# First attention interleaved with the 16 chunks of the attention gate and the recurrent output, tanh gates, queries laid out by fours

## The chip, the cores and the metric

The kernel runs on one core of a Trainium2 chip. The metric is the device time of one execution in microseconds (us), as the median of several runs. Engines are named as in the profile: PE (TensorE), DVE (VectorE), ACT (ScalarE), POOL (GpSimd), SP (SyncE, which only issues the loads here).

## The reference

A hybrid block for 256 tokens (with 16 meta tokens ahead of them T = 272), width 1024, and then a second block of two layers. Only the first half of the first block is touched:

```python
n1 = rmsnorm(h, norm1_g)
xr, gr, cq, ckv, kr, g_rnn, g_att = split(n1 @ w_in)
hr = rg_lru(causal_conv(xr))                        # linear recurrence over the tokens
y_rnn = (hr * gelu(gr)) @ w_rnn_out
q  = rmsnorm(cq)  @ w_uq                            # 16 heads, 64 nope + 32 rope
kv = rmsnorm(ckv) @ w_ukv                           # 16 heads, 64 key + 64 value
o  = causal softmax attention(q, k, v)              # rope on 32 of the 96 dims
y_att = o @ w_attn_out
mixed = sigmoid(g_rnn) * y_rnn + sigmoid(g_att) * y_att
h = h + mixed @ w_out
```

Behind it come a mixture over 16,384 experts (PEER) and the second block (four SwiGLU layers, a convolution module, an 8-head attention); they are the same before and after.

## The kernel before

All weights of all stages lie in one stream of 667 chunks of 128 x 1024 fp32 (512 KB each), in the order of `STAGES` (line 72). SP loads chunk c into slot c mod 3 of `raw`. ACT writes its rounded high half to `whi` (`split`, line 402) and DVE the remainder to `wlo` (`split`, line 830). PE then makes three passes per 128 x 128 tile (`passes`, line 1450): high times high, low activations, low weights. A chunk of a projection is 24 such matmuls into one PSUM bank (`chunk_out`, line 1463). PE adds one to `used` when it is done with a chunk, DVE adds one to `lo_done` when one is ready. Activations are split in the same way: ACT writes `XH`, DVE writes `XL`.

Every engine runs its own program in the written order, and the programs are tied by semaphores alone. The order around the change is: xr, ckv, kr, cq, gr (projections of n1), 16 small products for the recurrence gates, grnn (8 chunks, sigmoid on ACT, and between them on ACT and DVE the decay arithmetic of the recurrence, `decay`, line 542), gatt (8 chunks, beside them DVE's scans, line 1026), wro (recurrent output, 8 chunks), uq (queries: 16 heads of nine matmuls, line 597 on), uk (keys), uv (values), attention 1, wao (attention output), wout.

In uq a head's 128 outputs are 64 nope rows, 32 rope rows and the 32 rope rows turned. ACT copies the nope rows (line 571); DVE multiplies the rope rows by cosine (1049) and sine (1052) on 32 partitions and adds them (1054). POOL copies the rope rows of the keys for 16 heads (1881) behind the scans. In uv four banks of `wide` and two of `acc` collect the values; ACT copies them all out (585, 587) before attention begins. Projection outputs go through three banks `acc` in turn; `OUTS`, `EV` and `READ` (332 to 344) hold which engine has read each.

Attention 1 (1632 on PE, 1060 on DVE, 589 on ACT) treats a head as: two score matmuls (fp32, 96 rows; keys 144 and 272 wide), DVE adds the mask and takes the maximum (1072, 1077), ACT takes the exponential with its sum (598), DVE scales (1084, 1087), PE transposes five tiles (1656), ACT copies them (608, 610), PE multiplies by the values (1671). PE's order is scores(h+1), turn(h-1), values(h-2). No chunk is worked on meanwhile.

## Time and profile before

| | |
|---|---|
| median of 3 runs | 2295.47 us (2293.35 to 2297.09) |
| the profiled execution's own time | 2295.11 us |
| its span, first to last instruction | 2293.3 us |
| PE busy | 2184.4 us, 95% |
| DVE busy | 1548.8 us, 68% |
| ACT busy | 1189.1 us, 52% |
| first attention, on the trace's clock | about 227.4 to 322.3 us |

How to read it: all times in rows are microseconds from the span's start, unless marked ns. Busy time of PE counts a pipelined matmul from its start to its modelled end, so successive matmuls overlap; their rate is seen in the distance of their starts. PEclk is the clock that PE was granted, as a share of 2.4 GHz; 0.5 is 1.2 GHz. "Idle before" is followed by the instruction that ended most of the idle time.

### The profile page before, as it was taken

Reading aid. Unit: us, or ns where it says so; the run is one execution under the profiler, and the core shown is the slowest. Engines: PE = TensorE matmul, PEld = TensorE weight load, DVE = VectorE, ACT = ScalarE, POOL = GpSimd, SP = SyncE. Lnnn points to the kernel's source line nnn. Section 1 sums busy time; section 2 is a strip of 40 time slices with the busy share of each in tenths; the row PEclk is TensorE's granted clock in tenths of the full one; section 3 lists DMA queues with packets and bytes.
Section 4 is the critical chain, followed back from the end, with each engine's and each line's share of the span. In section 5 each row is a group of like instructions: output and inputs, shape, how many; then the busy total and the mean of one; then the engine's idle time right before and its main releaser. Section 6 shows DMA issues by size and latency. Waiting matters only on the chain.

```text
span 2293.3 us, 42218 instructions
## 1 busy us (share of the span) xinstructions
PE 2184.4 (95%) x15056; PEld 1976.8 (86%) x15056; DVE 1548.8 (68%) x2607; ACT 1189.1 (52%) x2009; POOL 52.1 (2%) x77
## 2 busy tenths in 40 slices
PE   7997899999999999999999999989999999979998
PEld 7896468999999998888888999978998999868997
DVE  6577445599989996555556666776666666656666
ACT  4765334565657675555555445535445444545444
POOL 0010000000010000000002000000000000000000
PEclk9999569999999999999999999999999999989999
DMA  5453015454543335555555666404554555424554
GB/s 197 151 171 117 1 52 176 151 182 168 185 160 120 128 127 187 194 193 193 194 193 175 236 223 205 148 28 166 187 183 152 193 184 182 165 74 137 185 186 142
DMA packets 100974, 366.35 MB, mean 160 GB/s; under 512 B 11488, under 2 KB 12000, under 8 KB 100384
## 3 DMA queue, kind: packets, MB, share of 16 engines
q1 hardware_dynamic: 97632, 352.46, 45.5%
q0 software_dynamic: 3264, 12.85, 1.5%
q8 instruction: 49, 0.80, 0.1%
q14 instruction: 29, 0.24, 0.0%
HBM read 363.16 MB, written 2.10 MB: 159 GB/s over the span
## 4 chain that ended last, share of the span: by engine, by line
PE 75%; DVE 13%; issue 5%; ACT 5%; DVEq 1%; DMA 0%; ACTq 0%
PE acc L1453 13%; PE acc L1455 12%; PE acc L1454 12%; PE wide L1756 8%; PE wide L1757 8%; PE wide L1758 8%; DVE wlo L834 2%; DVE arena L1239 2%; DVE res L1225 2%; ACT whi L413 1%; PE wide L1572 1%; PE wide L1574 1%; PE wide L1573 1%; PE sums L1671 1%; PE acc L1828 1%
## 5 line engine op out<-in xcount | busy, mean ns | idle before, releaser
L1453 PE MATMUL acc<-XH,whi 128*128 128x256 f32 (+1 forms) x3088 | 885.1, 287 | 16.1 <-DVE wlo L834 10.1
L1454 PE MATMUL acc<-XL,whi 128*128 128x256 f32 (+1 forms) x3088 | 874.9, 283 | 0.0
L1455 PE MATMUL acc<-XH,wlo 128*128 128x256 f32 (+1 forms) x3088 | 874.6, 283 | 0.0
L839 DVE TENSOR_TENSOR wlo<-raw,whi 128x1024 fp32r<-128x1024 f32 x396 | 484.8, 1225 | 302.5 <-ACT whi L418 282.5
L1453 PEld LDWEIGHTS acc<-XH,whi 128*128 128x128 f32 x3088 | 592.2, 192 | 28.3 <-DVE wlo L834 10.7
L1454 PEld LDWEIGHTS acc<-XL,whi 128*128 128x128 f32 x3088 | 592.5, 192 | 3.0
L1455 PEld LDWEIGHTS acc<-XH,wlo 128*128 128x128 f32 x3088 | 592.4, 192 | 0.0
L418 ACT ACTIVATE whi<-raw 128x1024 fp32r<-128x1024 f32 x456 | 479.8, 1053 | 181.3 <-PE wide L1758 181.0
L834 DVE TENSOR_TENSOR wlo<-raw,whi 128x1024 fp32r<-128x1024 f32 x268 | 328.1, 1227 | 171.2 <-ACT whi L413 160.6
L1756 PE MATMUL wide<-whi,small 128*128 128x512 f32 x864 | 338.4, 392 | 6.5 <-DVE wlo L834 3.6
L1757 PE MATMUL wide<-whi,small 128*128 128x512 f32 x864 | 337.8, 391 | 0.0
L1758 PE MATMUL wide<-wlo,small 128*128 128x512 f32 x864 | 336.6, 390 | 0.0
L413 ACT ACTIVATE whi<-raw 128x1024 fp32r<-128x1024 f32 x208 | 217.7, 1052 | 112.0 <-PE wide L1574 40.5
L1756 PEld LDWEIGHTS wide<-whi,small 128*128 128x128 f32 x864 | 162.8, 188 | 39.0 <-DVE wlo L834 4.4
L1758 PEld LDWEIGHTS wide<-wlo,small 128*128 128x128 f32 x864 | 162.6, 188 | 34.7
L1757 PEld LDWEIGHTS wide<-whi,small 128*128 128x128 f32 x864 | 162.9, 189 | 30.6
L706 ACT ACTIVATE arena<-arena 128x256 f32<-128x256 f32 x88 | 36.8, 418 | 193.2 <-DVE arena L1297 193.2
L712 ACT ACTIVATE small<-arena 128x256 fp32r<-128x256 f32 x88 | 36.7, 418 | 178.8 <-DVE arena L1306 178.8
L656 ACT ACTIVATE last_parts<-res,r2T 128x128 bf16<-128x128 bf16 x256 | 81.7, 390 | 58.3 <-DVE res L1225 58.3
L631 ACT ACTIVATE arena<-acc 128x256 f32 (+1 forms) x79 | 30.3, 383 | 93.8 <-PE acc L1455 93.6
L1308 DVE TENSOR_TENSOR small<-arena,small 128x256 fp32r<-128x256 f32 x88 | 37.6, 427 | 42.5 <-ACT small L712 42.5
L1297 DVE TENSOR_TENSOR arena<-acc,rstd 128x256 f32<-128x256 f32 x88 | 37.4, 425 | 39.8 <-PE acc L1455 39.4
(266 smaller groups left out, 2258.3 us busy)
## 6 DMA issues: line engine op xcount, KB each, us to landing
raw<-stream SPq DMA_DIRECT2D x664, 512.0 KB, 3.3
arena<-taps_in POOLq DMA_DIRECT2D x20, 256.0 KB, 4.0
arena<-rows_in POOLq DMA_DIRECT2D x7, 512.0 KB, 4.4
arena<-h_in SPq DMA_DIRECT2D x2, 544.0 KB, 4.4
res<-rgw SPq DMA_DIRECT2D x1, 1024.0 KB, 8.6
res<-tokens_in POOLq DMA_DIRECT2D x1, 1024.0 KB, 5.3
park<-res POOLq DMA_DIRECT2D x1, 1024.0 KB, 4.4
res<-park POOLq DMA_DIRECT2D x1, 1024.0 KB, 5.6
```

The source lines that it names most:

```text
L413: act.activation(whi[:, c % RING, :], raw[:, c % RING, :], ACT.Copy).then_inc(hi_done, 1)
L418: act.activation(whi[:, c % RING, :], raw[:, c % RING, :], ACT.Copy).then_inc(hi_done, 1)
L656: ins = act.activation(last_part(m % 2)[:, a, :], of_group(onehots, m % 2, 0)[:, a, 0, :], ACT.Copy, scale=r2T[:, bass.ds(4 * g + a, 1)])
L834: V.tensor_tensor(wlo[:, c % RING, :], raw[:, c % RING, :], whi[:, c % RING, :].bitcast(F32), ALU.subtract).then_inc(lo_done, 1)
L839: V.tensor_tensor(wlo[:, c % RING, :], raw[:, c % RING, :], whi[:, c % RING, :].bitcast(F32), ALU.subtract).then_inc(lo_done, 1)
L1225: V.tensor_tensor(pairs(onehots[:, s, 0, :]), of_tokens(e12, g), pairs(iotab[:, :]).to_broadcast([P, 8, NK // 2, 2]), ALU.is_equal)\
L1453: mm(out_, whi[:, s, w], xh, start=first, stop=False, **kw)
L1454: mm(out_, whi[:, s, w], xl, start=False, stop=False, **kw)
L1455: return mm(out_, wlo[:, s, w], xh, start=False, stop=last, **kw)
L1756: mm(dst, xh[:, x], whi[:, c % RING, w], start=first, stop=False, skip_group_check=True)
L1757: mm(dst, xl[:, x], whi[:, c % RING, w], start=False, stop=False, skip_group_check=True)
L1758: ins = mm(dst, xh[:, x], wlo[:, c % RING, w], start=False, stop=last, skip_group_check=True)
```

## The change

- The stream's order becomes grnn, uq, uk, uv, gatt, wro. The ckv norm moves into grnn; its halves lie in `small`, not in `XH` and `XL`.
- A loop of 18 steps replaces gatt, wro and attention: in step p PE does chunk p of the 16 of gatt and wro, then scores(p+1), turn(p-1) and values(p-2). ACT and DVE have the matching order. Scores alternate between two banks of `wide` (head 0 uses `sums`), transposes use the other two, values always use `sums`. The recurrent product y is written over `GR`, and its halves are made in step 7.
- The scans of the recurrence run in uv (two) and in steps 0 to 5.
- sigmoid(x) becomes (tanh(x/2) + 1)/2: ACT computes tanh, DVE adds one within its product, and the factor 0.5 is applied when `wout` is added to the residual.
- The weights of uq are laid out so that four heads give one output of 4 x 32 rope rows, one of the same rows turned, and two of 2 x 64 nope rows. DVE multiplies the first two on 128 partitions and adds four times on 32; ACT copies the other two. Cosine and sine tables are repeated on 128 partitions, which adds one constant load (128 KB).
- Key copies go to ACT and DVE by turns; the middle part of the values is copied by DVE. POOL's rope copies of the keys start before the square root of the recurrence, not behind its scans.
- The storage in `arena` is laid out anew, and the second attention's code is written out for itself, with the same instructions.

```diff
-STAGES = [("xr", 8), ("ckv", 2), ("kr", 1), ("cq", 3), ("gr", 8), ("grnn", 8), ("gatt", 8),
-          ("wro", 8), ("uq", 6), ("uk", 2), ("uv", 2), ("wao", 8), ("wout", 8), ("wq", 16),
+STAGES = [("xr", 8), ("ckv", 2), ("kr", 1), ("cq", 3), ("gr", 8), ("grnn", 8), ("uq", 6), ("uk", 2),
+          ("uv", 2), ("gatt", 8), ("wro", 8), ("wao", 8), ("wout", 8), ("wq", 16),
...
+        def score_bank(h):
+            return sums[:, :] if h == 0 else wide[:, h % 2, :]
+
+        def uv_bank(q):
+            return (GO["gatt"] + 1 + q) % RING
...
-        CKH, CKL = xt(XH, 384, 2), xt(XL, 384, 2)
+        CKH = small[:, 0:768].rearrange("p (t n) -> p t n", n=384)
+        CKL = small[:, 768:1536].rearrange("p (t n) -> p t n", n=384)
         CQH, CQL = xt(small, SEQ, 3), cl
         norm("n1", h0, DT, T, "norm1", 0, XHT, XLT)
         norm("cq", CQ, 3, SEQ, "qn", 0, CQH, CQL)
-        xsplit("yin", DT, SEQ)
         norm("ckv", CKV, 2, T, "kvn", 0, CKH, CKL)
+        xsplit("yin", DT, SEQ, sem("gated_y"), GR)
...
-                             ("rg", 16, "A"), ("grnn", 8, "A"), ("gatt", 8, "A"), ("wro", 8, "V"),
-                             ("uq", H1, "V"), ("uk", 8, "A"), ("wao", 8, "V"),
+                             ("rg", 16, "A"), ("grnn", 8, "A"), ("uq", 16, "VVAA"), ("uk", 8, "AV"), ("gatt", 8, "A"),
+                             ("wro", 8, "V"), ("wao", 8, "V"),
...
+                if k == 1:
+                    do_norm("ckv", split_later=True)
                 if k == 4:
                     act.wait_ge(sem("u_sq"), 1)
                     act.activation(HR, HR, ACT.Sqrt, scale=-1.0).then_inc(sem("u_root"), 1)
-            lin("grnn", lambda k, ps: act.activation(SG[:, k, :], ps, ACT.Sigmoid), between=decay)
-            lin("gatt", lambda k, ps: act.activation(SA[:, k, :], ps, ACT.Sigmoid))
-            act.wait_ge(used, BASE["gatt"] + 8)
-            do_xsplit("yin")
-            do_norm("ckv", split_later=True)
-            for k in range(DT):
-                split(BASE["wro"] + k + AHEAD)
-                if k == 5:
                     norm_root("ckv")
-
-            act.wait_ge(used, BASE["wro"] + 8)
...
+            for n in range(16):
+                if n % 3 == 0:
+                    split(BASE["uq"] + n // 3 + AHEAD)
+                if n % 4 >= 2:
+                    act.wait_ge(*output_ready("uq", n, 3))
+                    m, h = bank("uq", n), 4 * (n // 4) + 2 * (n % 4 - 2)
+                    act.activation(Q1[0:64, h, :], m[0:64, 0:SEQ], ACT.Copy, scale=SCALE1)
+                    act.activation(Q1[0:64, h + 1, :], m[64:128, 0:SEQ], ACT.Copy, scale=SCALE1).then_inc(outputs_read["A"], 1)
+            act.wait_ge(used, BASE["uq"] + 6)
             do_xsplit("ckv")
...
+            exps(0)
             act.wait_ge(used, BASE["uv"] + 2)
-            for t in range(2):
-                act.activation(V1[:, t, :], wide[:, 2 * t:2 * t + 2, :], ACT.Copy).then_inc(sem("v1"), 1)
+            act.activation(V1[:, 0, :], wide[:, 0:2, :], ACT.Copy).then_inc(sem("v1"), 1)
             for q in range(2):
-                act.activation(V1[0:META, 2, q * 512:(q + 1) * 512], acc[q][0:META, :], ACT.Copy).then_inc(sem("v1"), 1)
+                act.activation(V1[0:META, 2, q * 512:(q + 1) * 512], acc[uv_bank(q)][0:META, :], ACT.Copy).then_inc(sem("v1"), 1)
+            b = BASE["gatt"]
+            for p in range(18):
+                if 1 <= p <= 8:
+                    act.wait_ge(used, b + p)
+                    act.activation(SA[:, p - 1, :], bank("gatt", p - 1)[:, 0:SEQ], ACT.Tanh, scale=0.5).then_inc(READ["gatt"], 1)
+                if p < 16:
+                    split(b + p + AHEAD)
+                if p == 7:
+                    act.wait_ge(used, b + 8)
+                    do_xsplit("yin")
+                if 1 <= p <= 16:
+                    turned_probs(p - 1)
+                if p < 15:
+                    exps(p + 1)
...
+                if k == 6:
+                    norm_x("ckv")
...
+            qt = arena[:, XN + 2 * T:XN + 2 * T + SEQ * 2].rearrange("p (t n) -> p t n", n=SEQ)
+            for n in range(16):
+                if n % 3 == 0:
+                    split(BASE["uq"] + n // 3 + AHEAD)
+                if n % 4 < 2:
+                    dve.wait_ge(*output_ready("uq", n, 3))
+                    if n >= 4:
+                        dve.wait_ge(sem("q1"), n // 4 * 4)
+                    V.tensor_tensor(qt[:, n % 4, :], bank("uq", n)[:, 0:SEQ], (cos4, sin4)[n % 4], ALU.mult)\
+                        .then_inc(outputs_read["V"], 1)
+                if n % 4 == 1:
+                    dve.wait_ge(*OUTS[GO["uq"] + n])
+                    for i in range(4):
+                        V.tensor_tensor(Q1[64:96, n // 4 * 4 + i, :], qt[32 * i:32 * i + 32, 0, :], qt[32 * i:32 * i + 32, 1, :],
+                                        ALU.add).then_inc(sem("q1"), 1)
+            x_lo("ckv")
...
+                if j % 2:
+                    dve.wait_ge(*output_ready("uk", j, 2))
+                    m = bank("uk", j)
+                    V.tensor_copy(K1[0:64, 2 * j, :], m[0:64, 0:T])
+                    V.tensor_copy(K1[0:64, 2 * j + 1, :], m[64:128, 0:T]).then_inc(outputs_read["V"], 1)
...
+            def scores(h):
+                dve.wait_ge(sem("a1sc"), h + 1)
+                for t in range(2):
+                    m = 2 * h + t
+                    s, w, at = m % 4, KEYS["a1"][t], 0 if t == 0 else META + P
+                    if h >= 2:
+                        dve.wait_ge(sem("a1ptr"), h - 1)
+                    V.tensor_tensor(PR[:, s, 0:w], score_bank(h)[:, at:at + w], mask1[:, t, 0:w], ALU.add).then_inc(sem("a1sr"), 1)
+                    dve.wait_ge(sem("a1sr"), m + 1)
+                    V.tensor_reduce(tiny[:, 8 + s:9 + s], PR[:, s, 0:w], AX, ALU.max, negate=True).then_inc(sem("a1negmax"), 1)
+
+            def probs(h):
+                for t in range(2):
+                    m = 2 * h + t
+                    s, w = m % 4, KEYS["a1"][t]
+                    dve.wait_ge(sem("a1exp"), m + 1)
+                    link(V.reciprocal(tiny[:, 48 + s:49 + s], tiny[:, 12 + s:13 + s]))
+                    V.tensor_scalar(PR[:, s, 0:w], PR[:, s, 0:w], tiny[:, 48 + s:49 + s], None, ALU.mult).then_inc(sem("a1pr"), 1)
+
+            def pair_out(g):
+
+                dve.wait_ge(sem("a1pv"), 2 * g + 2)
+                V.tensor_copy(O1[:, g, :], sums[:, 0:SEQ]).then_inc(sem("x_full"), 1)
+            scores(0)
+            only_split("uv")
+            scan(0)
+            scan(1)
+            probs(0)
+            dve.wait_ge(used, BASE["uv"] + 2)
+            V.tensor_copy(V1[:, 1, :].rearrange("p (a n) -> p a n", a=2), wide[:, 2:4, :]).then_inc(sem("v1_middle"), 1)
+            b = BASE["gatt"]
+            for p in range(18):
+                if p < 15:
+                    scores(p + 1)
+                if p == 7:
+                    x_lo("yin")
+                if p < 16:
+                    split(b + p + AHEAD)
+                if p < 6:
+                    scan(p + 2)
+                if p >= 9 and p <= 16:
+                    k = p - 9
+                    dve.wait_ge(READ["grnn"], EV["grnn"] + DT)
+                    dve.wait_ge(used, b + p)
+                    V.scalar_tensor_tensor(out=SG[:, k, :], in0=SG[:, k, :], scalar=1.0, in1=bank("wro", k)[:, 0:SEQ],
+                                           op0=ALU.add, op1=ALU.mult).then_inc(READ["wro"], 1)
+                if p < 15:
+                    probs(p + 1)
+                if p >= 3 and p % 2:
+                    pair_out((p - 3) // 2)
...
+            for j in (6, 7):
+                pe.wait_ge(*OUTS[GO["uk"] + j])
+            pe.wait_ge(sem("q1"), H1)
+            pe.wait_ge(sem("k1_rows"), H1)
+
+            def scores(h):
+                if h >= 3:
+                    pe.wait_ge(sem("a1sr"), 2 * h - 2)
+                elif h >= 1:
+                    pe.wait_ge(sem("v1"), 1)
+                for t in range(2):
+                    w, at = KEYS["a1"][t], 0 if t == 0 else META + P
+                    ins = mm(score_bank(h)[:, at:at + w], Q1[0:96, h, t * P:(t + 1) * P], K1[0:96, h, 0:w], start=True, stop=True)
+                ins.then_inc(sem("a1sc"), 1)
+
+            def turn(h):
+                if h == 0:
+                    pe.wait_ge(sem("v1_middle"), 1)
+                else:
+                    pe.wait_ge(sem("a1pt"), h)
+                pe.wait_ge(sem("a1pr"), 2 * h + 2)
+                for t in range(2):
+                    m = 2 * h + t
+                    for kt in range(-(-KEYS["a1"][t] // P)):
+                        w = min(P, KEYS["a1"][t] - kt * P)
+                        at = (kt % 2) * SEQ + t * P
+                        ins = nc.tensor.transpose(wide[0:w, 2 + kt // 2, at:at + P], PR[:, m % 4, kt * P:kt * P + w], ident[:, :])
+                ins.then_inc(sem("a1ptr"), 1)
+
+            def values(h):
+                pe.wait_ge(sem("a1pt"), h + 1)
+                g, r0 = h // 2, (h % 2) * 64
+                if h == 0:
+                    pe.wait_ge(sem("a1sr"), 2)
+                    pe.wait_ge(sem("v1"), 3)
+                elif h % 2 == 0:
+                    pe.wait_ge(sem("x_full"), norms["o1"].full + g)
+                parts = [(0, P, 0, 2), (1, META, 0, 1), (1, P, 1, 1), (2, META, 1, 1)]
+                for n, (kt, w, t, nt) in enumerate(parts):
+                    ins = mm(sums[r0:r0 + 64, t * P:(t + nt) * P], V1[0:w, kt, h * 64:(h + 1) * 64],
+                             PT[0:w, h % 2, kt * SEQ + t * P:kt * SEQ + (t + nt) * P], start=kt == 0, stop=n in (1, 3),
+                             skip_group_check=True)
+                ins.then_inc(sem("a1pv"), 1)
+            scores(0)
             pe.wait_ge(sem("pad"), 2)
             tokens_out("uv", "ckv", [[wide[:, 0, :], wide[:, 1, :]], [wide[:, 2, :], wide[:, 3, :]],
-                                     [acc[0][:, :], acc[1][:, :]]], None)
-
-            def attention(tag, heads, nkt, n, Q, K, V, rows):
-                pr = ar(pr_at, n, 4) if tag == "a1" else ar(12288, n, 4)
-                pt = ar(pt_at, 768, 2) if tag == "a1" else ar(13312, 512, 2)
-                keys_of = KEYS[tag]
+                                     [acc[uv_bank(0)][:, :], acc[uv_bank(1)][:, :]]], None)
+            n1, b = norms["n1"], BASE["gatt"]
+            for p in range(18):
+                if p < 16:
+                    pe.wait_ge(lo_done, b + p + 1)
+                    free("gatt", p)
+                    if p in (1, 2):
+                        pe.wait_ge(sem("v1"), 3)
+                    hi, lo = (n1.hi[:, :, META:T], n1.lo[:, :, META:T]) if p < 8 else (XHS, XLS)
+                    chunk_out(bank("gatt", p)[:, 0:SEQ], b + p, hi, lo, "yin" if p == 8 else None).then_inc(used, 1)
+                if p < 15:
+                    scores(p + 1)
+                if 1 <= p <= 16:
+                    turn(p - 1)
+                if p >= 2:
+                    values(p - 2)
...
-            pool.wait_ge(sem("lru_done"), DT)
+            pool.wait_ge(sem("u_sq"), 1)
...
-    uq = np.concatenate([uq, turned(uq[..., NOPE:])], axis=-1).reshape(QL, H1 * P)
+    rope = uq[..., NOPE:].reshape(QL, 4, 4 * ROPE)
+    swapped = turned(uq[..., NOPE:]).reshape(QL, 4, 4 * ROPE)
+    uq = np.concatenate([rope, swapped, uq[..., :NOPE].reshape(QL, 4, 4 * NOPE)], axis=-1).reshape(QL, H1 * P)
```

## Rows read from the trace of the kernel before

**Rows 1.** the page: PE's granted clock in 40 slices, in tenths.

```profile
PEclk9999569999999999999999999999999999989999
```

**Rows 2.** windows by stage: us, busy of PE PEld DVE ACT POOL, PEclk, DMA.

```profile
100.20:129.20 29.00, 24.94 (x195) 24.32 (x193) 15.57 (x11) 26.89 (x29) 0.67 (x1) 0.94 0.41 146
129.20:152.50 23.30, 22.96 (x192) 22.76 (x192) 18.75 (x24) 10.46 (x17) 0.00 (x0) 1.00 0.60 204
152.50:177.10 24.60, 24.07 (x196) 23.91 (x197) 18.76 (x27) 13.19 (x21) 10.53 (x16) 1.00 0.53 172
177.10:205.00 27.90, 20.79 (x147) 17.95 (x145) 26.02 (x53) 12.04 (x24) 0.50 (x2) 1.00 0.32 109
205.00:215.90 10.90, 7.04 (x48) 6.16 (x48) 6.58 (x10) 8.37 (x20) 0.00 (x0) 1.00 0.40 133
215.90:227.40 11.50, 8.45 (x36) 6.68 (x36) 2.45 (x2) 4.95 (x7) 0.00 (x0) 1.00 0.35 115
227.40:322.30 94.90, 85.90 (x273) 43.23 (x273) 37.38 (x135) 34.61 (x106) 0.00 (x0) 0.56 0.00 1
```

**Rows 3.** timeline of PE (start, us): heads at either clock.

```profile
227.45 3.11 PE L1643 MATMUL wide<-arena 96*128 96x144 f32 x12 [3.05 <-ACT arena L587]
242.10 1.68 PE L1671 MATMUL acc<-arena 128*64 128x256 f32 x7
243.71 0.97 PE L1643 MATMUL wide<-arena 96*128 96x144 f32 x4
247.39 2.96 PE L1671 MATMUL sums<-arena 128*64 128x256 f32 x8
250.28 1.76 PE L1643 MATMUL wide<-arena 96*128 96x144 f32 x4
251.83 1.27 PE L1656 MATMUL acc<-ident,arena 128*128 128x128 f32 x5
```

**Rows 4.** timeline of PE: two chunk matmuls at the low clock.

```profile
323.05 0.41 PE L1481 MATMUL acc<-XH,wlo 128*128 128x256 f32 x1
323.26 0.41 PE L1480 MATMUL acc<-XH,whi 128*128 128x256 f32 x1
```

**Rows 5.** timeline of POOL and DVE: rope copies, subtractions, a reciprocal.

```profile
152.66 10.53 POOL L1881 COPY arena<-arena 32x272 f32<-32x272 f32 x16 [50.89 <-DVE arena L1026]
152.97 4.47 DVE L846 TENSOR_TENSOR XL<-arena,XH 128x256 fp32r<-128x256 f32 x8
174.77 1.85 DVE L856 RECIPROCAL rstd<-rstd 128x272 f32<-128x272 f32 x1
322.69 2.77 DVE L846 TENSOR_TENSOR XL<-arena,XH 128x256 fp32r<-128x256 f32 x8
```

**Rows 6.** groups by line, query stage: busy, mean ns, idle before.

```profile
L1453 PE MATMUL acc<-small,whi 128*128 128x256 f32 x48 | 14.9, 310 | 7.0 <-DVE arena L1052 6.4
L1052 DVE TENSOR_TENSOR arena<-acc,zone 32x256 f32<-32x256 f32 x14 | 6.0, 428 | 0.2
```

**Rows 7.** timeline of ACT in grnn; PE's first gate matmul.

```profile
103.30 0.39 ACT L554 ACTIVATE arena<-acc 128x256 f32<-128x256 f32 x1 [1.37 <-PE acc L1455]
103.58 2.02 ACT L545 ACTIVATE arena<-arena 128x2176 f32<-128x2176 f32 x1
...
117.09 1.28 ACT L554 ACT_TABLE_LOAD   x1
...
120.01 1.28 ACT L553 ACT_TABLE_LOAD   x1
...
129.17 0.39 PE L1453 MATMUL acc<-XH,whi 128*128 128x256 f32 x1 [0.52 <-DVE wlo L834]
```

**Rows 8.** windows around two changes of PE's clock.

```profile
116.00:119.60 3.60, 1.21 (x10) 1.22 (x11) 2.49 (x2) 3.57 (x5) 0.00 (x0) 1.00 0.09 15
119.70:123.00 3.30, 3.30 (x17) 3.30 (x17) 2.10 (x2) 3.27 (x4) 0.00 (x0) 0.50 0.43 154
242.60:245.90 3.30, 2.08 (x11) 1.11 (x10) 1.98 (x7) 0.76 (x3) 0.00 (x0) 1.00 0.00 0
```

314 lines of the change are left out of this document (143 added, 171 removed).

## The prediction

> **What bounds the kernel now.** I read the page first, then a table of windows over the stages that the change touches, then the PE instructions inside attention. The page says that PE is busy 95% of the span, and that its granted clock is 0.9 or 1.0 of full nearly everywhere [rows 1]: most of the 2293.3 us is TensorE at full rate, which only fewer or faster matmuls would shorten. The slices with clock 5 and 6 stand out. The windows [rows 2] place them: in the first attention (227.40 to 322.30, 94.9 us) PE is busy 85.90 us but at a mean clock of 0.56, so at the 1.2 GHz level for nearly all of it, while DVE (37.38) and ACT (34.61) are mostly idle and no weights are moved. The same rows show two smaller losses: the query projection (uq, 177.10 to 205.00) has PE busy 20.79 of 27.9 us beside a DVE busy 26.02, and the stage of values (215.90 to 227.40) PE busy 8.45 of 11.5. Everything after 322.3 is the same work in the same order, so the forecast is the sum over the 222.1 us from 100.2 to 322.3.
>
> **Attention between chunks.** Per head PE does three groups. At the low clock the starts in [rows 3] give: values 247.39 to 250.28, 2.89 us; scores 250.28 to about 251.95, 1.67; five transposes from 251.83, 1.1. That is 5.65 us a head, times 16 is 90.4 of the 94.9; the rest is waiting. One stretch fell into the high clock: seven of the eight records of the values took 1.68 us and the scores 0.97. I take, at full clock, values 1.6, scores 0.92, transposes 0.55 and 0.15 for re-filling the weights after the three semaphore waits: 3.2 us a head. Lower end: half of 5.65, 2.8; upper 3.4.
> A chunk is 24 matmuls that start 0.12 apart: 192 in the 23.3 us of the gate stage [rows 2] is 2.86 us each, and 0.1 for the wait ahead of it. So a step of chunk and head is 6.2 us (5.7 to 6.4). Sixteen steps are 99.2; the first head's scores (0.9) have moved ahead of the values stage, and at the end one head's transposes, its copy on ACT and its values stand alone, some 2.5 us with the waits. Sum 100.8. Before: 23.3 + 24.6 + 94.9 = 142.8. **Saved 42.0.**
> This needs three things. First, DVE and ACT must fit in a step. A head costs DVE 37.38/16 = 2.3 us and ACT 34.61/16 = 2.2 [rows 2]; what they did beside a gate chunk is 18.75/8 = 2.3 for DVE (split, scan, product) and 10.46/8 = 1.3 for ACT. Sum 4.7 for DVE and 3.5 for ACT against 6.2 for PE. Second, the order must leave slack. DVE starts a step with scores(p+1), which wait for PE's scores behind the chunk and, because a probability slot must be free, for turn(p-1): about 4.5 us into the step. Then come the split of chunk p+2, a scan, and probs(p+1), done some 9.3 us after the step began; PE wants them in turn(p+1), two steps on, at 12.4 + 3.9. The split is done near 7.1 and wanted at 12.4. So a delay of up to 5 us on DVE is hidden; it costs in full only beyond that. At p = 7 ACT's eight copies and DVE's eight subtractions for the recurrent output enter: 2.8 us of DVE work [rows 5] started about 3 us before chunk 8 and consumed at the same pace, so I count under 0.5 us. Third, the clock, below.
>
> **Values stage.** PE waits 3.05 us for ACT's copies before the first scores [rows 3]. Now gate chunk 0 goes to the third bank and starts at once; it and the scores behind it cover ACT's copies and DVE's copy of the middle part. Scores(0) now run before the stage, so exponentials and probabilities of head 0 hide under its 36 matmuls. 11.5 becomes 8.3: **saved 3.2.** If DVE were late with its copy, turn(0) in step 1 is what waits, 6 us later.
>
> **Queries for four heads.** Today each head costs DVE two products and an addition on 32 partitions, 0.43 us each, and PE waits for the second product [rows 6]: a head every 1.45 us plus a split of 1.22 every third. Four heads now take two products over 128 partitions, four additions (back to back about 0.35 each, as eight subtractions took 2.77 [rows 5]) and 1.3 splits: 0.9 + 1.5 + 1.6 = 4.0 us on DVE; ACT has four copies of 0.39 (as a product of the same width takes it [rows 7]) and 1.3 splits, 3.0; PE four outputs of nine matmuls at 0.12 and a wait each, 4.6. Four groups would be 18.4. But the ckv norm now stands on DVE just ahead (reciprocal 1.85 [rows 5], two multiplies 0.9), between the splits of the first two uq chunks: the second is late by some 1.5 us, the first eviction by 2. I take 22.0 instead of 27.9: **saved 5.9** (ends 3 and 8.5).
>
> **Keys.** The hi and lo halves of ckv are made only once the last query output has read that storage: 1 us of new wait. The 16 copies go to ACT and DVE by turns instead of ACT alone, and PE's 48 matmuls take 6.1; 0.6 for the last copies, 0.9 for scores(0). 8.6 for 10.9: **saved 2.3** (0 to 3).
>
> **The stage before (grnn, 29.0 us).** It is bound by ACT, which is busy 26.89. Sigmoid makes it switch tables around each exponential; with tanh three loads of 1.28 go (one is the load at 117.09 [rows 7]) if tanh and exp share a table, and the squares (0.75) and the root (0.5) of the ckv norm come in. Two loads less and the squares let the second exponential end 1.8 earlier, and with it DVE's multiply that the square root waits for. The load at 120.01 ran 0.7 past that multiply; it will be hidden, and the root costs 0.5: the split behind comes 2.0 earlier. But the 16 GpSimd copies of rope rows now run here, not behind the scans. [Rows 5] show what they do: eight subtractions beside them took 4.47 us against 2.77 elsewhere, 0.21 more each. Four DVE instructions meet them before the next stage's first chunk is split, 0.8 us. So PE starts that stage at 128.0 instead of 129.17 [rows 7]: **saved 1.2** (−3 to 3).
> The Trainium skill (SBUF — State Buffer, "Who interferes with whom") says that a VectorE instruction with two SBUF inputs and a GpSimd instruction that reads SBUF lock each other out for a whole instruction. With 16 copies in 10.53 us a copy is 0.66 [rows 5], so the rule allows four times 0.66 = 2.6 us here and the time would be 1.8 us later; the trace agrees that they disturb each other, but its mean of 0.21 stays in the sum.
>
> **Small things.** One more constant load of 128 KB lies among loads issued 10 us before they are needed; a scalar_tensor_tensor for a tensor_tensor in 20 places is within 0.06 us each. I take 0.
>
> **Sum.** 42.0 + 3.2 + 5.9 + 2.3 + 1.2 = 54.6. The profiled execution took 2295.11 us (span 2293.3 and 1.8 around it); its median over three runs is 2295.47, the same within 0.4. So 2240.5; I say 2241. With the ends of the terms (attention 45 to 34, queries 3 to 8.5, grnn −3 to 3) this case alone spans 2232 to 2250.
>
> **Rivals.**
> *A, the clock drops for parts of the loop.* Attention alone did not hold the high level: it came at 242.6, for 3.3 us with PE busy 2.08 of them, and went again [rows 8]. Now each head (3.2 us) is followed by 2.9 us of dense matmuls. For holding: the query stage kept 1.00 with PE busy 20.79 of 27.9 us [rows 2]. For dropping: in grnn 3.6 us in which PE was busy only 1.21 were followed by 3.3 us at 0.50 [rows 8]. Each microsecond at the low level loses half a microsecond of work. My estimate for this case is a third of the loop low, 34 us: 17 us, 2258.
> *B, tanh and exp do not share a table.* In steps 1 to 8 ACT would load twice (2.57): 3.5 + 2.6 = 6.1, as much as PE; two steps' slack gone, about 5 us, and grnn's 3.8 lost: 2250. For sharing: Tanh ran behind Sigmoid without a load [rows 7], but no row has it behind Exp. The Trainium skill (ScalarE: Activation LUTs, "Table sets: the hidden batching unit") lists tanh in the set of exp, which is against this rival.
> *C, the order on DVE is the bound.* DVE is 4.7 of 6.2 only by busy time; with semaphore waits in the middle of the queue it could be 7.2 a step: +16, 2257. Against it: the slack computed above.
> *D, slower than before.* One mechanism: the clock stays low through the loop, as it did in attention. Then the chunks too run at 1.2 GHz, 24 matmuls at 0.213 [rows 4] = 5.1 us, and a step is 5.1 + 5.65 = 10.8: 4.6 more than counted, times 16 = 74, so 2241 + 74 = 2315. It decides from 12 of 16 steps low (12 × 4.6 = 55). Against it: every stage that holds dense chunks and waits under 10 us shows 0.94 or 1.00 [rows 2].
>
> **How the numbers follow.** Forecast (all steps at the high clock, PE the bound, 2232 to 2250) 0.62; A 0.18; B 0.05; C 0.10; D 0.03; 0.02 for nothing gained. The range takes the forecast's and most of A and C: 2231 to 2262, holding 0.8. Within 0.2% (4.6 us, what a measurement of this kernel can tell from none) is 0.02; slower 0.03, faster 0.95.
>
> **What would show it.** A loop of 16 chunks about 100 us long, starting near 167 on the trace's clock, with PE busy over 95% and clock 1.00; wait rows of PE for DVE's probabilities near zero; ACT without table loads in it; uq near 22 us with DVE at about 80%; no PE gap behind the values stage. Wrong if the clock in the loop is under 0.9 (A, D), if loads appear there (B), or if chunks or transposes wait for DVE (C).

## The result, and the profile after

The changed kernel took 2232.12 us (median of four, 2231.29 to 2237.25) against 2294.41 for the kernel before beside it: ratio 0.9733, 95% interval 0.9714 to 0.9751. Timed again beside the last experiments it took 2230.99 against 2295.14, ratio 0.9727 (0.9714 to 0.9741). Forecast were 2241 and a range from 2231 to 2262. So the direction held, and the time lies at the lower edge of the range (the second median 0.01 us below it): the gain, 62 to 64 us, is 8 to 10 us larger than the 54.5 forecast. Of all executions one is left out below: one of the second kernel of experiment 4, which took 4650.32 us where its three others took 2231.42 to 2239.77.

The page of the changed kernel: busy time of PE, and the row that answers to [rows 1].

```profile
PE 2148.1 (96%) x15056; PEld 1964.7 (88%) x15056; DVE 1538.7 (69%) x2592; ACT 1177.0 (53%) x1995; POOL 52.6 (2%) x77
...
PEclk9999999999999999999999999989999999979999
```

The slices with 5 and 6 are gone. The windows by stage answer to [rows 2]: grnn, uq, uk, scores(0) with uv, the loop of 18 steps, and two short stretches in uq and uk. Columns as in [rows 2].

```profile
100.60:127.54 26.94, 24.90 (x198) 23.60 (x197) 15.89 (x11) 24.18 (x29) 9.22 (x11) 1.00 0.46 157
127.54:151.84 24.30, 19.76 (x144) 18.97 (x145) 21.30 (x36) 12.90 (x25) 3.02 (x9) 0.91 0.44 152
151.84:162.26 10.42, 9.12 (x49) 8.74 (x49) 6.12 (x11) 5.40 (x11) 0.00 (x0) 0.72 0.40 124
162.26:171.22 8.96, 8.96 (x41) 7.46 (x42) 5.23 (x9) 1.97 (x5) 0.00 (x0) 1.00 0.31 103
171.22:266.17 94.95, 94.23 (x654) 74.24 (x652) 67.49 (x178) 52.73 (x133) 0.00 (x0) 1.00 0.27 94
133.80:137.20 3.40, 3.40 (x18) 3.40 (x17) 2.89 (x6) 0.88 (x3) 0.00 (x0) 0.50 0.62 212
150.90:157.70 6.80, 5.86 (x26) 5.89 (x27) 3.25 (x7) 2.65 (x6) 0.00 (x0) 0.50 0.49 154
```

The loop does in 94.95 us what gatt, wro and attention did in 142.8, at clock 1.00 and with PE idle for 0.72 us in all. From grnn's first matmul to the loop's end it is 165.57 us for 222.07, 56.5 saved. The last two rows were not forecast: two stretches at 0.50, in the query and key stages.

One step of the loop in the changed kernel's timeline (columns as in [rows 3]). The values of one head come first, then a chunk (its first matmul is shown), scores, transposes, and the next head's values.

```profile
188.90 1.72 PE L1739 MATMUL sums<-arena 128*64 128x256 f32 x8
189.75 0.41 ACT L609 ACTIVATE arena<-arena,tiny 128x144 f32<-128x144 f32 x1
190.55 0.38 PE L1528 MATMUL acc<-XH,whi 128*128 128x256 f32 x1
191.09 0.36 ACT L627 ACTIVATE arena<-acc 128x256 f32<-128x256 f32 x1
193.49 0.87 PE L1712 MATMUL wide<-arena 96*128 96x144 f32 x4
194.20 0.71 PE L1726 MATMUL wide<-ident,arena 128*128 128x128 f32 x5
194.84 0.65 PE L1739 MATMUL sums<-arena 128*64 128x256 f32 x2
```

Values 1.65, chunk 2.94, scores 0.71, transposes 0.64: 5.94 us from values to values. The tanh of the gate (ACT L627) stands between exponentials (L609) without a table load.

The execution shown took 2237.25 us. Of the kernel's nine executions one other took about as long (2236.69); the seven others took 2229.08 to 2232.64. A second profiled execution, the one of 2229.08, shows the difference. Its windows of grnn, uq, uk and the loop:

```profile
98.19:125.14 26.95, 24.87 (x198) 23.57 (x197) 15.90 (x11) 24.23 (x29) 9.23 (x11) 1.00 0.47 157
...
125.14:147.93 22.79, 18.29 (x144) 17.49 (x145) 21.11 (x36) 12.85 (x25) 3.02 (x9) 1.00 0.49 162
147.93:155.81 7.88, 6.51 (x49) 6.11 (x49) 6.13 (x11) 5.40 (x11) 0.00 (x0) 1.00 0.50 170
164.77:259.73 94.96, 94.24 (x654) 74.29 (x652) 67.48 (x178) 52.69 (x133) 0.00 (x0) 1.00 0.28 94
```

The clock did not fall: the query stage is 1.51 us shorter and the key stage 2.54, everything else in the stretch equal within 0.02. In this execution the stretch is 161.5 us, 60.5 less than before. It also reached grnn 2.4 us earlier, again mostly by the clock: from 70 us on it needs 28.19 us to grnn, at a clock of 1.00, where the first took 30.60 at 0.94 (the kernel before took 30.17, also at 0.94). The last 1.8 us lie behind the loop. The mean clock of a whole execution tells the two kinds apart: 0.982 and 0.983 in the two long ones, 0.985 to 0.990 in the seven short.

### The profile page after: what moved, and what is told of

Its sections match the earlier page's. It is cut to its first block, busy times and chain, and to the rows that moved or that the text cites. A ratio compares the mean times of both kernels' runs of the same rounds, so it can differ in the third digit from the quotient of the medians.

```text
span 2235.5 us, 42151 instructions
## 1 busy us (share of the span) xinstructions
PE 2148.1 (96%) x15056; PEld 1964.7 (88%) x15056; DVE 1538.7 (69%) x2592; ACT 1177.0 (53%) x1995; POOL 52.6 (2%) x77
## 4 chain that ended last, share of the span: by engine, by line
PE 77%; DVE 13%; issue 5%; ACT 4%; DVEq 1%; DMA 0%; ACTq 0%
PE acc L1528 13%; PE acc L1530 13%; PE acc L1529 13%; PE wide L1876 9%; PE wide L1877 8%; PE wide L1878 8%; DVE wlo L879 3%; DVE arena L1314 2%; DVE res L1300 2%; ACT whi L435 1%; PE wide L1647 1%; PE wide L1648 1%; PE wide L1649 1%; PE acc L1948 1%; PE sums L1739 1%
## 5 line engine op out<-in xcount | busy, mean ns | idle before, releaser
L1878 PEld LDWEIGHTS wide<-wlo,small 128*128 128x128 f32 x864 | 162.2, 188 | 34.3
L1877 PEld LDWEIGHTS wide<-whi,small 128*128 128x128 f32 x864 | 162.5, 188 | 30.5
```

The costliest lines, as they stand in the source:

```text
L1877: mm(dst, xl[:, x], whi[:, c % RING, w], start=False, stop=False, skip_group_check=True)
L1878: ins = mm(dst, xh[:, x], wlo[:, c % RING, w], start=False, stop=last, skip_group_check=True)
```

## Experiments

Eleven edited kernels ran, and the changed kernel once more. Each time is a median, with the ratio to the kernel before timed on the same chip; the changed kernel's is 0.973. Line numbers are each kernel's own and differ by a few.

**1. The clock alone, in the kernel before.**

```diff
                 def turn(h):
                     if h >= 1:
                         pe.wait_ge(sem(tag + "pt"), h)
+                    if tag == "a1":
+                        for _ in range(20):
+                            mm(acc[1][:, 256:384], iotab[:, :], iotab[:, :], start=True, stop=True)
```

> The kernel before with nothing of the change: in the first attention each head's TensorE work gets 20 more bf16 products of 128 x 128 x 128 into a part of a PSUM bank that nobody reads, between the head's scores and its turn of the probabilities; they change no result. At full rate they are 1.1 us a head (20 x 0.057), at half rate 2.3. Theory (what the heads lost before was TensorE's clock: 94.9 us of the attention at a mean granted clock of 0.56): TensorE is fed while it would wait for the exponentials, the clock stays near 1.0, and the attention takes 70 to 86 us in spite of the added work, so the kernel is 9 to 25 us faster than before. Rival (what the heads lost was the order, each waiting for its own exponentials and sums): the attention is longer by 18 to 37 us and the kernel slower by as much.

Measured: 2273.28 against 2296.10, ratio 0.9898 (0.9881 to 0.9914): 23 us faster with 320 more matmuls. The window of its attention:

```profile
226.87:300.92 74.05, 72.09 (x592) 47.79 (x592) 37.39 (x135) 33.41 (x103) 0.00 (x0) 0.98 0.01 1
```

94.9 us became 74.05 at a clock of 0.98. A head takes 4.6 us, about 1.1 of them for the added products (from 237.98 to 239.10 in one head), where it took 5.9: the heads' loss was the clock. The added products also fill most of PE's waits (1.6 us are left of 9.0), so this run does not say what held the clock down. The Trainium skill (TensorE: Matmul & The Clock Gate, "Part 1: The HAM clock gate") says that activity of the engine is what releases its throttle; this run agrees, 0.56 to 0.98 by work that nobody reads.

**2. The interleaving undone, in the changed kernel.** All chunks first, then all heads; and, as a middle way, groups of four.

```diff
+ORDER = [("C", p) for p in range(17)] + [("H", p) for p in range(18)]       # apart
+ORDER = [(x, p) for n in range(5) for x in "CH" for p in range(4 * n, 4 * n + 4)
+         if p < (17 if x == "C" else 18)]                                    # fours
...
-            for p in range(18):
+            for part, p in ORDER:        # on PE, ACT and DVE alike: each part keeps its instructions
```

> The changed kernel with its 16 chunks of the attention gate and of the recurrent output all ahead of the first head, and the heads behind them; the instructions, the buffers, the gates as tanh and the query layout stay. It undoes the interleaving alone. Theory (the interleaving is most of the gain, since it keeps TensorE fed and its clock up between a head's steps): the 35 steps take 138 to 142 us where the loop took 95, the clock in the heads falls to about 0.56, and the kernel is 42 to 47 us slower than the changed one, near 2277. Rival (the gain comes from the other parts: the tanh gates, the layout, the copies spread over engines): the loop stays under 110 us and the kernel is less than 15 us slower than the changed one.

> The changed kernel with the loop in groups: four chunks, then four heads, and so on; the same instructions. Theory (a chunk between two heads is needed, for the heads' own gaps bring the clock down within one group of about 12 us): the groups of heads run in part at a clock of 0.5 and the loop takes 105 to 120 us, the kernel 10 to 25 us slower than the changed one. Rival (any chunk work near by keeps the clock up, and the heads' waits for their exponentials are short at full clock): the loop takes 95 to 100 us and the kernel is within 5 us of the changed one.

Measured: apart 2240.82, ratio 0.9760 (0.9744 to 0.9776); fours 2240.29, 0.9756 (0.9740 to 0.9772). Windows of the chunks and of the heads, apart:

```profile
171.00:218.57 47.57, 46.23 (x386) 45.84 (x385) 33.19 (x50) 23.35 (x35) 0.00 (x0) 1.00 0.52 176
218.57:272.00 53.43, 50.61 (x271) 29.22 (x269) 36.80 (x129) 30.68 (x98) 0.00 (x0) 0.97 0.03 11
```

and the 18 steps in fours:

```profile
168.11:271.19 103.08, 99.41 (x653) 77.23 (x651) 69.70 (x178) 53.72 (x133) 0.00 (x0) 0.95 0.26 87
```

My theory fell. Without any chunk between them, sixteen heads take 53.43 us at a clock of 0.97, 3.3 a head; those of before took 5.9 [rows 2]. Undoing the interleaving costs 6.1 us of the 47.8 that the loop saved (47.57 + 53.43 = 101.00 against 94.95), in fours 8.1. In each of the two kernels the clock falls once in the heads, and each time behind a wait of PE for VectorE's copy of a finished pair: 1.23 us apart (the clock is 0.57 from 232 to 236), 2.21 us in fours (0.58 from 210 to 220). Something else in the changed heads keeps the clock, and one difference is VectorE's order. The next two kernels ask for it.

**3. One line of VectorE's order, in the kernel before.** It scales head h's probabilities in step h, not in step h + 1; only the last head's scaling stays late.

```diff
                 for h in range(heads + 2):
                     if h < heads:
                         scores(h)
-                    if 1 <= h <= heads:
+                        if tag == "a1" and h < heads - 1:
+                            probs(h)
+                    if h == heads or tag == "a2" and 1 <= h < heads:
                         probs(h - 1)
```

> The kernel before with one line of VectorE's program moved: in the first attention it scales a head's probabilities right behind that head's mask and maximum (as the changed kernel does), no longer a step later behind the next head's mask and maximum; only the last head stays late, so that the order of its PSUM bank holds. No chunk lies between the heads. The changed kernel with its chunks apart from its heads ran the heads at full clock, at 3.2 us each, where those of before took 5.9 at half clock. Theory (the late scaling makes TensorE wait 0.7 to 1.5 us for it in each pair of heads, and these waits hold the clock at half): the waits go, the clock comes back to 1.00 within some heads, and the attention takes 50 to 70 us instead of 94.9, the kernel 25 to 42 us faster than before. Rival (what matters is how the heads begin: 3 us of idle TensorE and a table load ahead of the first head of before, none in the changed kernel, and a clock once low stays low): the attention takes 85 to 95 us, at a mean clock under 0.65, the kernel 0 to 10 us faster.

Measured: 2254.40 against 2294.69, ratio 0.9824 (0.9808 to 0.9840): 40 us faster. First its window of attention, then PE's waits in it (us in total, times, longest), then PE's groups for one head and the next start, and the last head's transposes.

```profile
227.06:283.15 56.09, 54.36 (x273) 31.51 (x273) 38.05 (x135) 32.96 (x106) 0.00 (x0) 0.91 0.00 1
```

```profile
PE wide L1645 <- ACT arena L587: 3.1, 1, 3.1
PE acc L1658 <- DVE arena L1087: 1.0, 1, 1.0
PE acc L1658 <- ACT arena L610: 0.7, 1, 0.7
```

```profile
235.35 0.97 PE L1645 MATMUL wide<-arena 96*128 96x144 f32 x4
236.15 0.71 PE L1658 MATMUL acc<-ident,arena 128*128 128x128 f32 x5
236.79 1.72 PE L1673 MATMUL acc<-arena 128*64 128x256 f32 x8
238.45 0.97 PE L1645 MATMUL wide<-arena 96*128 96x144 f32 x4
...
276.13 1.30 PE L1658 MATMUL acc<-ident,arena 128*128 128x128 f32 x5 [1.01 <-DVE arena L1087]
```

Attention 56.09 us for 94.9, a head in 3.10 us. It begins as before does, behind 3.05 us of idle PE and a table load: in both kernels the clock is 1.00 at first and falls within 1.5 us. Here it is back at 1.00 near 232 and stays there until the one head that is still scaled late: PE waits 1.01 us for it, and from 276.5 to the end the clock is 0.50. What the moved line took away is seen in the kernel before, in rows that the prediction did not read. PE's waits in attention:

```profile
PE acc L1656 <- DVE arena L1087: 9.0, 9, 1.5
```

The timeline of one wait at the high clock, then of a pair of heads at the low clock:

```profile
246.16 1.30 PE L1656 MATMUL acc<-ident,arena 128*128 128x128 f32 x5 [1.48 <-DVE arena L1087]
...
253.03 2.96 PE L1671 MATMUL sums<-arena 128*64 128x256 f32 x8
255.93 1.76 PE L1643 MATMUL wide<-arena 96*128 96x144 f32 x4
256.04 0.42 DVE L1100 COPY arena<-sums 128x256 f32<-128x256 f32 x1 [6.14 <-PE sums L1671]
...
258.34 0.36 DVE L1087 TENSOR_SCALAR arena<-arena,tiny 128x272 f32<-128x272 f32 x1
258.38 1.30 PE L1656 MATMUL acc<-ident,arena 128*128 128x128 f32 x5 [0.69 <-DVE arena L1087]
```

And windows between two of the short rises of its clock and in the second:

```profile
246.20:266.40 20.20, 19.51 (x59) 9.82 (x60) 7.19 (x26) 6.40 (x21) 0.00 (x0) 0.50 0.01 2
266.40:269.70 3.30, 2.00 (x10) 1.05 (x10) 2.06 (x8) 0.84 (x3) 0.00 (x0) 0.99 0.00 0
```

VectorE stands 6.14 us in its queue at the copy of a finished pair (L1100), which waits for that pair's values. Only behind it come the next head's mask and maximum, and only behind these the scaling of the head whose transposes PE wants next: 2.4 us from the end of the values, in which PE has only the scores. At half clock the scores take 1.76 of it and PE waits 0.69; when the clock comes up they take 0.97 [rows 3] and PE waits 1.48. So whenever the clock rose, PE met a longer wait, and the clock was low behind it: three rises of 3.3 us (from 242.6 [rows 8], 266.4 and 290.2), 23.8 us apart, each ending in a wait of 1.48. This tells how each rise ended. It does not tell why the clock then stayed low: from 246.16 to 257.69 PE had no wait (busy 11.52 of 11.53 us) and its clock was 0.50 throughout. That VectorE's order is the cause is shown by the run; that it acts through the waits alone is not.

**4. Late scaling in the changed kernel,** with the chunks apart and in the loop.

```diff
-                if p < 15:
-                    probs(p + 1)
+                if 1 <= p < 16:
+                    probs(p)
```

> The changed kernel with its chunks ahead of its heads (as in the run before) and, in addition, VectorE's scaling of a head's probabilities a step later, behind the next head's mask and maximum, as the kernel before had it. Theory (late scaling is what holds the clock of the heads at half): the heads take 5 to 6 us each at a clock near 0.5 and the kernel is 25 to 45 us slower than with the chunks apart alone (2240.8), 2266 to 2286. Rival (the heads begin at full clock behind the chunks and stay there): within 6 us of 2240.8.

> The changed kernel, chunks and heads step by step as they are, with VectorE's scaling of a head's probabilities a step later. Theory (2.9 us of chunk between two heads give VectorE time for it either way: the interleaving is a cover that makes the order harmless): within 3 us of the changed kernel's 2232. Rival (the turn of the probabilities comes right behind the next scores and waits for VectorE in every step): 0.5 to 1.5 us a step, 8 to 24 us slower, more if the clock falls.

Measured: apart 2244.66, ratio 0.9787 (0.9765 to 0.9808); in the loop 2236.86 (median of three), 0.9741 (0.9715 to 0.9767). The heads apart, then the loop:

```profile
213.10:267.40 54.30, 51.11 (x270) 27.58 (x268) 35.63 (x129) 30.83 (x98) 0.00 (x0) 1.00 0.03 11
```

```profile
171.15:267.95 96.80, 94.60 (x654) 74.11 (x652) 67.73 (x178) 52.73 (x133) 0.00 (x0) 1.00 0.28 92
```

With the chunks apart the theory fell and the rival held (3.8 us above the 2240.8 by the medians, 6 by the ratios): late scaling alone does not bring the low clock back. In the loop the theory held by the trace and by the ratio: late scaling costs 1.85 us there (96.80 against 94.95), and 0.9741 and 0.9733 lie within each other's intervals; the chunk covers it. The two orders differ from that of before in one more place, which I had overlooked when I wrote the expectation: in the changed kernel VectorE runs a head further ahead of TensorE, so the copy of a finished pair asks for values that are a step older. In the rows of the kernel apart it does not wait (the first row is PE's longest wait in these heads):

```profile
217.83 0.74 PE L1732 MATMUL wide<-ident,arena 128*128 128x128 f32 x5 [1.83 <-DVE arena L1125]
...
237.31 0.36 DVE L1125 TENSOR_SCALAR arena<-arena,tiny 128x272 f32<-128x272 f32 x1
237.59 0.42 DVE L1130 COPY arena<-sums 128x256 f32<-128x256 f32 x1
```

What stands: in the kernel before, the chain copy, mask, scaling, transposes keeps the clock down, and cutting it at the scaling (3) gives 38.8 us of the 94.9. In the changed kernel neither the chunks between the heads nor the early scaling is needed for the clock: without both it is 1.00, even behind a wait of 1.83 us. What is left of the difference from before is the copy, which VectorE does not wait for there except at the end, the PSUM banks and semaphores of the heads as they were rewritten, and the start: these heads follow the chunks at once, while those of before start behind 3.05 us of idle PE and lose the clock 1.5 us later. No run separates these; (3) shows only that with the start of before the clock can come back.

**5. Gates as sigmoid, in the changed kernel.** Only the function and the constants behind it change.

```diff
-ACT.Tanh, scale=0.5)
+ACT.Sigmoid)
...
-scalar=1.0, in1=bank(...), op0=ALU.add, op1=ALU.mult)
+scalar=0.0, in1=bank(...), op0=ALU.add, op1=ALU.mult)
```

> The changed kernel with its gates as sigmoid again (in the place and order of the changed kernel; the products behind them take the sigmoid as it is, so the number of instructions is unchanged). Theory (the gates as tanh are there because a sigmoid and an exponential in one step need two loads of function tables): steps 1 to 8 of the loop get two loads of about 1.3 us each on ScalarE, beside 5.95 us of TensorE work in a step; ScalarE becomes what the step waits for in these eight, at 0.3 to 2 us a step, so 3 to 15 us slower than the changed kernel. Rival (ScalarE has room for both loads beside TensorE's 5.95 us): within 2 us of the changed kernel.

Measured: 2240.09, ratio 0.9757 (0.9741 to 0.9774); its profiled execution 2231.93. In that one ACT loads twice in each of steps 1 to 8 (two of its 16 loads, from the timeline), yet the window of the loop is only 0.35 us longer.

```profile
173.32 1.28 ACT L627 ACT_TABLE_LOAD   x1
...
176.58 1.28 ACT L609 ACT_TABLE_LOAD   x1
```

```profile
167.46:262.76 95.30, 94.28 (x654) 74.25 (x652) 69.03 (x178) 72.57 (x149) 0.00 (x0) 1.00 0.27 94
```

Its grnn stage, in which it loads six times for three, takes 30.5 us (97.83 to 128.30) for 26.94. So the tanh is worth 3.5 us in grnn and 0.4 in the loop. In the loop the rival was right; the kernel's median lies in the theory's range, but for another reason. It is 8 us above the changed kernel's, and the 4 beyond these 3.9 go with the clock: the profiled execution ran at a mean clock of 0.990, the three others (2239.94 to 2240.45) at 0.982 or 0.983. Compared at the same clock it is 2231.93 against the changed kernel's 2229.08 at 0.990, and 2240.2 against 2237.0 (means) at 0.982 to 0.983: 3 us either way. Whether sigmoid makes the falls more frequent, three of four for two of nine, so few executions can't tell.

**6. Queries head by head, in the changed kernel:** weight columns and read-outs as before, three VectorE instructions a head instead of six for four.

> The changed kernel with its queries laid out and read out of PSUM head by head as before (the columns of the weight in the old order; VectorE three instructions a head, ScalarE one). It undoes the query layout alone. Theory (the layout shortens VectorE's chain in the query stage): the stage takes 27 to 28 us where the changed kernel took 24.3, the kernel 3 to 6 us slower than the changed one's 2232. Rival (the stage is bounded by the splits of its weights or by TensorE, and what the layout gave is lost at once to waits in the keys' stage): within 1.5 us of 2232.

Measured: 2247.77, ratio 0.9798 (0.9782 to 0.9815), 15 us slower than the changed kernel: both the theory and the rival missed. A group and a timeline row of its query stage (PE waits 5.7 us in it for VectorE's sine products, L1085), and the changed kernel's row that answers to the second:

```profile
L1523 PE MATMUL acc<-small,whi 128*128 128x256 f32 x48 | 15.6, 326 | 7.9 <-DVE arena L1085 5.7 <-DVE wlo L876 0.9 <-ACT arena L579 0.9
```

```profile
161.03 0.57 PE L1523 MATMUL acc<-small,whi 128*128 128x272 f32 x1 [5.12 <-DVE small L888]
```

```profile
151.84 0.57 PE L1528 MATMUL acc<-small,whi 128*128 128x272 f32 x1 [2.50 <-DVE small L891]
```

The stage takes 34.3 us (126.76 to 161.03) for 24.3, and not 27.9 as before: the halves of ckv now stand in VectorE's queue behind the last query (5.12 us of wait for 2.50), the norm's instructions between the first splits. From the first query to scores(0) it is 44.68 us for 34.72, or for 30.67 in the execution whose clock did not fall. Here the clock falls in both stages (0.89 and 0.71), and the mean clock of all four executions is 0.980 to 0.982: in the new order of stages the layout is worth 10 us beside a changed kernel with the falls, 14 beside one without. Either is more than the 3.6 by which this stage beats the old one.

**7. The two waits that are left, in the changed kernel.**

```diff
 # norm early: ahead of ScalarE's wait for the product of the decay, and two splits earlier on VectorE
+                    norm_root("ckv")
...
-                    norm_root("ckv")
...
-                if k == 6:
+                if k == 4:
 # ckv first: ahead of the read-outs of the last query group; x_lo("ckv") on VectorE likewise
+                if n == 15:
+                    act.wait_ge(used, BASE["uq"] + 6)
+                    do_xsplit("ckv")
...
-            act.wait_ge(used, BASE["uq"] + 6)
-            do_xsplit("ckv")
```

> The changed kernel with the two halves of the compressed keys made ahead of the last query group's read-outs on ScalarE and VectorE, not behind them. TensorE waits 2.50 us for the second half at the head of the keys' stage, and in the profiled execution its clock is at half for 6.8 us right behind. Theory (the wait is that order, and the clock falls by it): the wait shrinks to about 1 us and the clock stays up, 1.5 us by the wait and up to 3.4 by the clock in those executions that have the fall, so 1.5 to 5 us faster than the changed kernel. Rival (the query group's read-outs are then late by as much, and the scores of head 0 with them): within 1 us of it.

> The changed kernel with the root of the compressed keys' norm taken ahead of ScalarE's wait for the queries' sums, and the norm's products two splits earlier on VectorE. TensorE waits 0.86, 0.90 and 0.97 us at the head of the query stage, and its clock is at half for 3.4 us right behind. Theory (VectorE's norm products between two splits delay the query weights): two of the three waits shrink, 1 to 2 us, and 1.7 us by the clock in those executions that have the fall, so 1 to 3.5 us faster than the changed kernel. Rival (the splits of the decay stage in front are late instead, and TensorE waits there): within 1 us, or up to 1 us slower.

> Both edits of the two runs before at once. Theory: the sum, 2.5 to 8 us faster than the changed kernel, near 2226, with a granted clock of 1.00 through the query and key stages. Rival (each edit only moves the wait): within 1 us of it.

> The changed kernel itself, unchanged, beside the three others on the same chip: 2231 to 2238 us. If the difference between its executions (2231.3 to 2237.3) is that of the clock's two falls in the query and key stages, an execution near 2237 shows both falls and one near 2231 shows at most one. Rival (it is noise from elsewhere, the transfers): no connection.

Measured, beside 2230.99 and 0.9727 for the changed kernel itself: ckv first 2231.50, 0.9723 (0.9709 to 0.9736); norm early 2229.79, 0.9714 (0.9700 to 0.9727); both 2228.77, 0.9712 (0.9699 to 0.9726). The intervals overlap, so no gain is measured. In the traces each edit did what it was made for: ckv first shortens the wait of 2.50 to 1.36, norm early removes those of 0.90 and 0.97 and adds 0.8 in grnn (1.18 for 0.42). But the clock does not follow the waits: it fell in both stages with ckv first (0.93 and 0.82), and in neither with norm early, where the wait of 2.49 was still there. The query and key stages of both, at clock 1.00, as in the execution of the changed kernel with 22.79 and 7.88:

```profile
125.77:145.06 19.29, 17.75 (x145) 17.38 (x145) 17.65 (x32) 11.10 (x22) 4.63 (x8) 1.00 0.59 192
145.06:153.69 8.63, 6.81 (x48) 6.18 (x49) 7.28 (x12) 7.29 (x14) 0.00 (x0) 1.00 0.44 149
```

27.92 us for 30.67, 2.75 less, of which grnn gives back 0.8 (PE waits 1.15 there for a split that stands behind the earlier norm, for 0.42): 2.0 by the traces, 2.2 by the medians. It is the fastest kernel here, by an amount that these rounds do not settle. On the falls of the clock: in the pair of profiles of the changed kernel the waits ahead of them are equal (0.90 and 0.97 against 0.88 and 0.96; 2.50 against 2.49), and the clock of one execution fell twice, that of the other not at all. The wait alone does not decide it. As expected, the long execution of this round (2236.69) has the lowest mean clock, 0.983, and the four short ones have 0.986 to 0.990; only the profiled one shows where.

## Why the prediction was right, and where not

**Attention between chunks (42.0 forecast, 47.8 measured).** Right in clock (1.00), bound (PE 94.23 of 94.95) and slack of the other engines. Too small in two terms. A head costs 3.00 us at full clock, not 3.2: the scores take 0.71, not 0.92, and no row shows the 0.15 taken for re-filling the weights as a term of its own; 16 times 0.2 are 3.2 us. And the 2.5 us added for the end counted the last head's transposes and values twice, for sixteen full heads were in the 99.2 already. A step was 5.94 for 6.2. The 47.8 also lie outside the ends given for this term, 45 to 34, which do not follow from its own steps: 5.7 to 6.4 us a step give 50 to 39.

But the step's reason was wrong, and only the experiments show it. I wrote of the 94.9 us that 90.4 were work at the low clock and "the rest is waiting", and that "attention alone did not hold the high level". The rest was nine waits for one VectorE instruction, 9.0 us, and the order of VectorE's queue behind them is what kept the clock low: with one line of it moved the same heads, alone, take 56.09. The interleaving is worth 6 to 8 us in the changed kernel, where I credited it with 42. Something in the rewritten heads, which the forecast did not price, keeps the clock there without it. The sum needed only a clock of 1.00, whatever brought it, so in this term the number came out by luck. Whether the interleaving would have brought the clock back with the heads of before, in their old order, no run shows.

**Values stage (3.2).** Right, 3.1: its matmuls run from 162.83 to 171.22, 8.39 us where 8.3 was forecast, and no wait follows them.

**Queries (5.9) and keys (2.3).** In the execution with the falls of the clock the queries saved 3.6 and the keys with scores(0), from 151.84 to 162.83, nothing; in the one without, 5.1 (22.79 for 27.9) and 2.5 (147.93 to 156.38, 8.45 where 8.6 was forecast). The four additions took 1.76 a group, not the 1.5 that I took from wider subtractions:

```profile
148.32 1.76 DVE L1091 TENSOR_TENSOR arena<-arena 32x256 f32<-32x256 f32 x4
```

and the wait for the halves of ckv was 2.50 where I had 1. The falls, which cost 4.0 us in the pair of executions above, I had not forecast outside the loop.

**grnn (1.2).** 2.06: of 0.8 us for POOL's copies beside VectorE, 0.3 came. Four instructions met them; the first three rows are three of these, the last the copies.

```profile
122.33 1.22 DVE L879 TENSOR_TENSOR wlo<-raw,whi 128x1024 fp32r<-128x1024 f32 x1 [2.28 <-ACT whi L435]
123.47 2.63 DVE L1069 TENSOR_TENSOR arena<-arena 128x2176 f32<-128x2176 f32 x1
126.13 1.31 DVE L879 TENSOR_TENSOR wlo<-raw,whi 128x1024 fp32r<-128x1024 f32 x1
...
118.98 9.08 POOL L2001 COPY arena<-arena 32x272 f32<-32x272 f32 x11 [16.78 <-DVE arena L1065]
```

Against 1.23 for a split without them and 2.42 for the same multiply in the kernel before, the excess is 0, 0.21 and 0.08; the fourth, a split at 118.83, took 1.22. The rule that the prediction named (the Trainium skill, SBUF — State Buffer, "Who interferes with whom") would have made it 2.6; these rows don't show a delay of a whole copy (0.83 here).

**The sum.** 54.6 were forecast for the stretch; 56.5 were measured in the execution with falls of the clock in the query and key stages, 60.5 in the one without. (The ends of the terms, all low at once, give 2256 and not the 2250 of the forecast.) The rest of the gain lies outside the stretch: in the second execution 2.0 us ahead of it and 3.5 behind. It belongs to no term of the change: ahead, the kernel before and the first execution have a fall of the clock that the second lacks (0.94 for 1.00, as above); behind, the kernel of experiment 3 is 2.3 us shorter too, with the program of before.

**Rivals.** A and D: the clock in the loop was 1.00. B: no load between the loop's tanh and exponentials. The Trainium skill (ScalarE: Activation LUTs, "Table sets: the hidden batching unit") lists tanh in the set of exp, and this trace agrees. The rival's price was too high in the loop, 0.4 us measured for 5, and right in grnn, 3.5 for 3.8. C: VectorE is busy 67.49 of 94.95, and PE waits for it 0.7 us in all.

## What to carry to other kernels

Where TensorE runs a stage at half clock, look first for the short waits inside it (here nine, 9 of 95 us) and for who ends them: moving one step of one queue was worth 40 us here. Ask of a copy that frees a PSUM bank what stands behind it in its engine's queue. Before crediting one part of a change with a clock that came back, undo that part by itself: here it was worth 6 of 48 us. And profile a kernel twice: between two executions of one program falls of the clock came and went, worth some 6 of the 8 us between them.

## What the runs showed of the hardware

- The same program with the same waits (within 0.02 us) ran once with two falls of TensorE's clock, 3.4 and 6.8 us long, and once with none; that is 4.0 of the 8.2 us between its two profiled executions.
- A wait of 1.83 us was followed by no fall of the clock (experiment 4, apart); waits of 1.01 us (experiment 3), 1.23 and 2.21 us (experiment 2) were each followed by one.
- 320 matmuls of 128 columns whose output is never read made a stage 21 us shorter (74.05 for 94.9, clock 0.98 for 0.56).
- Eight steps with two table loads each (2.57 us) beside 5.9 us of TensorE work cost 0.35 us in all: ACT was busy 72.57 of 95.30.
